# Hybrid trunk with routed experts: pair 2 is routed one phase ahead, hgrn groups start 20 slots apart, the router reads the unscaled residual, attention's steps stand two slots apart

## Chip, core and metric

One NeuronCore of a Trainium2 chip. The metric is the device time of one execution in microseconds (us), the median of several.

## What is computed

256 positions of 1024 float32 features pass through two layers, each a token mixer followed by a routed feed-forward (PEER), and a final RMSNorm.

```python
def reference(x, ...):
    h = x
    for i in range(2):
        xn = rmsnorm(h, mixer_norm[i])
        h = h + (swa_attention if i == 0 else hgrn2)(xn, ...)
        h = h + peer_ffn(rmsnorm(h, ffn_norm[i]), peer_w_q[i], peer_sub_keys[i], peer_u[i], peer_v[i])
    return rmsnorm(h, final_norm)

def peer_ffn(xn, w_q, sub_keys, u_tab, v_tab):        # per block of 128 positions
    q = (xb @ w_q).reshape(128, 8, 2, 128)             # 8 heads, 2 halves
    s = einsum('phcd,hckd->phck', q, keys)             # 128 scores per half
    sv, si = top_k(s, 16)
    cv, ci = top_k(sv[:, :, 0, :, None] + sv[:, :, 1, None, :], 16)   # of 16 x 16 sums
    expert = i1 * 128 + i2                             # indices picked by ci
    gates = softmax(cv)
    act = gelu(einsum('pd,phkd->phk', xb, u_tab[expert]))
    return einsum('phk,phkd->pd', gates * act, v_tab[expert])
```

So each position reads 8 x 16 = 128 experts per layer, each a u row and a v row. Attention is grouped-query with rotary positions and sinks; hgrn2 is a gated linear recurrence, here in 7 levels of doubling blocks.

## The kernel before

The 256 positions are two tiles of 128 (`TILES`). Work runs in four **phases** of 128 **slots** (`PER`). A slot `n` is one expert of each of the 128 rows of the phase's tile (phases 0 and 2: tile 0, layers 0 and 1; phases 1 and 3: tile 1).

The **foreground** of a slot goes through all engines. POOL (L386) issues an indirect DMA that gathers 128 rows of u and v (8 KB each) into one of the 8 slots of `ring`, once PE has freed slot n-8 (`slots_free`). DVE (L885) multiplies the u rows with `xn` and sums them up (`dots`); it waits for the landed gather. ACT takes gelu (L504), multiplies with the gate (`coef`) and makes a diagonal matrix (`diag`, L396). PE (L1212) multiplies that diagonal with the v rows and adds into `acc`, in two 512-wide matmuls, each run as two passes, so x4 in the trace. Then it increments `slots_free`.

**Beside** the foreground, each engine does the other work of the phase at written-out slot numbers: function `beside(p, q)` of each engine is called after `foreground` of slot q (on PE after that of slot q-1). Every engine is in order, so a wait in `beside` holds the foreground behind it. The other work is

- the *token mixer* of the other tile: attention in phase 0 (four groups, starts `ATTN_HEAD + 16 i`, step r of a group in slot start + r), hgrn in phases 1 and 2 (four groups, starts `HEAD + HGRN_PERIOD * i` = 8, 25, 42, 59). In a hgrn group PE projects at r = 0 to 13 (L1126 and L1130), ACT takes the sigmoid at r = 14 (L470), PE computes a level of scores at r = 16 to 23 (24 in phase 2, L1142), and the output projection runs at r = 33 to 36 (L1175). Weights come through `wmix`, issued by SP at r = 7, 14 (input, 2048 KB each) and 37 (output, 1024 KB).
- at `MIXED` = 96 DVE adds the mixer's output to `h` (`add_up`), the row is normalised (ACT squares, DVE `norm_ims`, ACT sqrt, DVE `norm_scale`), PE transposes `xn`, and ACT and DVE copy it to `xTs` (`norm_xT`).
- *routing* of the heads in five **units**: unit 0 is head 0, unit 1 head 1 (both routed in the last slots of the phase before), units 2, 3, 4 are pairs of heads. A unit is: PE projects (`route_project`, L1183, eight k-steps of 128x128 per column, a pair has four columns), ACT copies (`route_copy`), PE scores (L1202), DVE takes the top 16 per column (`top`), then the 256 sums, indices and gates (`candidates` to `gates`). `ROUTE_PE`, `ROUTE_SCORE`, `ROUTE_EXP`, `PAIR_DVE`, `HEAD_DVE` hold the slots. POOL waits for a head's indices (`r_done`) before its first gather. The routing weights of a unit (`wroute`, 2304 KB) are one buffer, reloaded by SP once the scores of the unit before are done (`load_route`).

At a phase boundary DVE adds `acc` to `h` in slot 1, once PE has done the last slot of the phase before; PE's first foreground waits for that (`h_ready`).

Before the phases stands a **prologue**: attention of tile 0, projections of tile 1 (`ahead`, from weights that lie in ring slots 0 to 5, so that gathers into these wait for it), the norm of tile 0 and the routing of units 0 and 1.

Of the kernel before, what the change touches and what calls it, by code (L numbers as in the profile page):

```python
# [13 lines left out]
P = 128  # L14
# [66 lines left out]
def trunk(nc, x, cos, sin, masks_attn, masks_hgrn, ident_in, iota_in, gains, mixer_gain, sinks, lb_raw, out_gain,  # L81
          attn_in, attn_out, hgrn_in, hgrn_out, route_w, experts, out):
    with ExitStack() as ctx:
# [16 lines left out]
        gainT = sb("gainT", [P, 2, KT])  # L100
# [17 lines left out]
        warm = sb("warm", [P, 2])  # L118

# [86 lines left out]
        xT_ps, xT_act, xT_dve, xT_mix = sem("xT_ps"), sem("xT_act"), sem("xT_dve"), sem("xT_mix")  # L206
# [67 lines left out]
        def rbank_of(u):  # L274
            return cbank if u % UNITS == 1 else rbank
# [10 lines left out]
        def _(sp):  # L286
# [60 lines left out]
            for p in range(PHASES):  # L347
                for q in range(PER):
                    if q == 10:
                        load_route(p, 2)  # L350
                    elif q == 26:
                        load_route(p, 3)
                    elif q == 50 and p == 1:
                        load_route(p + 1, 0)
                    elif q == 109 and p < 3:
                        load_route(p + 1, 1)
                    if p == 0:
                        if q == 37:
                            load_hgrn_in(0, 0, 0)
                        elif q == 69:  # L360
# [7 lines left out]
                    if q == 100 and p in (0, 2):  # L368
# [23 lines left out]
        def _(act):  # L392
# [95 lines left out]
            def route_copy(p, unit):  # L488
                u = unit_phase(p, unit) * UNITS + unit
                act.wait_ge(r_proj, u + 1)  # L490
                cols = scored(u)
                copy(rqT[:, cols], bands(rbank_of(u)[:], RHC)[:, cols]).then_inc(r_qT, 1)

            def route_exp(p, unit):
                u = unit_phase(p, unit) * UNITS + unit
                act.wait_ge(g_shift, u + 1)
                hs = heads_of(u)
                act.activation(ge[:, hs], cvs[:, hs], ACT.Exp).then_inc(g_exp, 1)
# [13 lines left out]
            def beside(p, q):  # L512
# [4 lines left out]
                elif q == 3 and p:  # L517
                    norm_sqrt(norm_at(p, 0))
# [858 lines left out]
```

## Time and profile before

| | us |
|---|---|
| runs shown, median (lowest, highest), 3 runs | 1582.83 (1579.26, 1584.77) |
| profiled execution | 1582.65 |
| its span, first to last instruction | 1580.6 |

| engine | busy us | share of the span |
|---|---|---|
| PE | 1380.6 | 87% |
| DVE | 1065.9 | 67% |
| ACT | 664.6 | 42% |
| POOL | 563.4 | 36% |

The DMA engines moved 628.01 MB, 397 GB/s over the span; the software queue with the gathers takes 82.5% of the 16 engines' time, SP's hardware queue 13.7%. In the page's 40 slices the DMA engines are at 9 tenths or more in all but the second and the last. How to read it: a share of the span is an average over stages with different limits, so the rows below go by stage. In a timeline row the columns are start, duration, engine, line, operation, and in brackets how long the engine had idled before it and who released it. An issue on POOL dates the release of the slot eight before.

### The profile page before, as it was taken

What the parts mean: (1) busy time and instruction counts of PE and PEld (TensorE: products, weight loads), DVE (VectorE), ACT (ScalarE), POOL (GpSimd) and SP (SyncE); (2) the same over time, 40 slices, a digit from 0 to 9 for tenths busy, and PEclk for the clock granted to TensorE, in tenths of its full rate; (3) what the DMA queues carried; (4) which work ended last, traced back from release to release, by engine and by line L of the source; (5) the groups of instructions that cost most, each with busy time, mean ns of one, the idle gap of its engine ahead of it and who ended that gap; (6) DMA issues with size and microseconds to landing.
All of it is one profiled execution on the core that took longest, in us unless ns stands there. A gap on an engine that the chain in (4) does not pass through costs nothing.

```text
span 1580.6 us, 15779 instructions
## 1 busy us (share of the span) xinstructions
PE 1380.6 (87%) x4918; PEld 739.3 (47%) x4918; DVE 1065.9 (67%) x2560; ACT 664.6 (42%) x1897; POOL 563.4 (36%) x518
## 2 busy tenths in 40 slices
PE   8899988878789989988878998999897888977776
PEld 5555554324246657543434665755452443422222
DVE  3369676665857677778585766688958585666644
ACT  3235445344443343454444334255444433344333
POOL 0033433444344223334433333242543344344441
PEclk9999998999999999999999999999999998999999
DMA  9099999999999999999999999999999999999995
GB/s 370 21 380 422 402 422 388 403 422 421 423 420 423 423 423 355 422 423 420 421 422 421 422 423 423 347 420 355 395 420 422 422 423 423 420 421 421 422 421 247
DMA packets 84051, 628.01 MB, mean 397 GB/s; under 512 B 9728, under 2 KB 10368, under 8 KB 13696
## 3 DMA queue, kind: packets, MB, share of 16 engines
q0 software_dynamic: 73728, 536.90, 82.5%
q1 hardware_dynamic: 9664, 89.87, 13.7%
q8 instruction: 38, 0.62, 0.2%
q10 hardware_dynamic: 576, 0.25, 0.1%
q14 instruction: 45, 0.37, 0.1%
HBM read 625.93 MB, written 1.05 MB: 397 GB/s over the span
## 4 chain that ended last, share of the span: by engine, by line
PE 44%; DMA 30%; DVE 13%; ACT 9%; issue 3%; POOL 0%; DVEq 0%; ACTq 0%; POOLq 0%
DMA ring<-experts,idx 30%; PE acc L1212 25%; DVE ring L885 7%; PE rbank L1183 5%; PE ab L1126 2%; PE ab L1130 2%; ACT L504 2%; PE acc L998 2%; PE y L1009 2%; ACT diag L396 1%; PE y L1175 1%; ACT coef L396 1%; PE cbank L1183 1%; ACT gel L504 1%; ACT L470 1%
## 5 line engine op out<-in xcount | busy, mean ns | idle before, releaser
L1212 PE MATMUL acc<-ring,diag 128*128 128x512 f32 x2048 | 994.5, 614 | 181.0 <-ACT diag L396 173.9
L386 POOL DMA_INDIRECT ring<-experts,idx x512 | 562.2, 1098 | 989.6 <-PE acc L1212 877.5
L885 DVE CUSTOM_DVE_ANT_0 ring<-ring,xn 128x1024 f32<-128x1024 f32 x512 | 624.3, 1223 | 302.5 <-DMA ring<-experts,idx 283.8
L1212 PEld LDWEIGHTS acc<-ring,diag 128*128 128x128 f32 x2048 | 362.6, 193 | 632.1 <-ACT diag L396 348.3
L504 ACT ACTIVATE gel<-dots 128x1 f32<-128x1 f32 x512 | 103.5, 202 | 770.0 <-DVE dots L885 769.2
L396 ACT ACTIVATE diag<-ident,coef 128x128 f32<-128x128 f32 x512 | 205.7, 402 | 16.8
L396 ACT ACTIVATE coef<-gate,gel 128x1 f32<-128x1 f32 x512 | 151.1, 295 | 16.6
L1183 PEld LDWEIGHTS rbank<-xTs,wroute 128*128 128x128 f32 x896 | 117.2, 193 | 49.2 <-issue 49.0
L1183 PE MATMUL rbank<-xTs,wroute 128*128 128x128 f32 x896 | 117.8, 276 | 0.9 <-DVE xTs L625 0.9
L1126 PEld LDWEIGHTS ab<-xTs,wmix 128*128 128x128 f32 x512 | 64.0, 192 | 10.5 <-issue 10.5
L1126 PE MATMUL ab<-xTs,wmix 128*128 128x128 f32 x512 | 67.6, 275 | 0.0
L1130 PE MATMUL ab<-wmix,xTs 128*128 128x256 f32 x256 | 63.1, 379 | 0.0
L504 ACT ACT_TABLE_LOAD x46 | 59.0, 1283 | 0.8
L1130 PEld LDWEIGHTS ab<-wmix,xTs 128*128 128x128 f32 x256 | 46.8, 190 | 15.6 <-issue 11.5
L885 DVE DVE_READ_ACCUMULATOR2_ANT dots<- 128x1 f32 x512 | 42.3, 83 | 0.0
L708 DVE TENSOR_TENSOR mix<-mix 128x512 f32<-128x512 f32 x48 | 33.2, 692 | 1.6
L1175 PE MATMUL y<-wmix,mix 128*128 128x512 f32 x64 | 33.0, 598 | 0.0
L998 PE MATMUL acc<-ring,xTs 128*128 128x384 f32 x96 | 32.5, 489 | 0.6 <-issue 0.6
L1009 PE MATMUL y<-wmix,mix 128*128 128x512 f32 x64 | 31.0, 597 | 0.5 <-ACT mix L396 0.5
L768 DVE MAX8 sv<-rbank 128x8 f32<-128x128 f32 x56 | 16.6, 296 | 20.8 <-PE rbank L1202 20.8
L1142 PEld LDWEIGHTS cbank<-mix 128*128 128x128 f32 x144 | 21.5, 192 | 15.3 <-issue 15.3
L724 DVE COPY_PREDICATED mix<-hmask,cbank 128x256 f32<-128x256 uint32 x32 | 14.1, 442 | 19.1 <-PE cbank L1142 13.8
(192 smaller groups left out, 916.0 us busy)
## 6 DMA issues: line engine op xcount, KB each, us to landing
wmix<-hgrn_in SPq DMA_DIRECT2D x16, 2048.0 KB
wroute<-route_w SPq DMA_DIRECT2D x14, 2304.0 KB
ring<-experts,idx POOLq DMA_INDIRECT x512
wmix<-hgrn_out SPq DMA_DIRECT2D x8, 1024.0 KB, 12.0
ring<-attn_in SPq DMA_DIRECT2D x3, 1536.0 KB, 8.6
wmix<-attn_out SPq DMA_DIRECT2D x4, 1024.0 KB, 10.1
ring<-attn_in SPq DMA_DIRECT2D x2, 768.0 KB, 8.4
gain<-gains SPq DMA_DIRECT2D x3, 512.0 KB
```

What stands on the lines that cost most here:

```text
L386: pool.indirect_dma_start(out=ring[:, k * 2 * D:(k + 1) * 2 * D], out_offset=None, in_=experts, in_offset=bass.IndirectOffsetOnAxis(ap=idx ...
L396: return act.activation(to, of, ACT.Copy, scale=scale)
L504: link(act.activation(gel[:, k:k + 1], dots[:, k:k + 1], ACT.Gelu))
L708: dve.tensor_tensor(to, hkq, sufpre, ALU.mult).then_inc(h_factors, 1)
L885: dve.tensor_tensor_reduce(out=u_rows(k), in0=u_rows(k), in1=xn[:, tile], scale=1.0, scalar=0.0, op0=ALU.mult, op1=ALU.add, accum_out=dots ...
L998: last = nc.tensor.matmul(to[:, 0:AW], xTs[:, side, k], w[:, k * AW:(k + 1) * AW], start=k == 0, stop=k == KT - 1)
L1009: last = nc.tensor.matmul(y[:, j * HALF:(j + 1) * HALF], a_oT[:, n % 2, c * P:(c + 1) * P], w[:, c * D + j * HALF:c * D + (j + 1) * HALF], ...
L1126: nc.tensor.matmul(ab[:, j, c * P:(c + 1) * P], w[:, k, c * P:(c + 1) * P], xTs[:, 0, k], start=k == 0, stop=k == KT - 1)
L1130: last = nc.tensor.matmul(ab[:, j, 256:512], xTs[:, 0, k], w[:, k, 256:512], start=k == 0, stop=k == KT - 1)
L1175: last = nc.tensor.matmul(y[:, j * HALF:(j + 1) * HALF], h_oT[:, c * P:(c + 1) * P], wmix[:, c, HIN + j * HALF:HIN + (j + 1) * HALF], star ...
L1183: last = nc.tensor.matmul(rbank_of(u)[:, c * P:(c + 1) * P], wroute[:, (k * RHC + c) * P:(k * RHC + c + 1) * P], xTs[:, 1, k], start=k == ...
L1212: last = nc.tensor.matmul(acc[:, j * HALF:(j + 1) * HALF], diag[:, n % DIAGS], v_rows(k)[:, j * HALF:(j + 1) * HALF], start=n % PER == 0, ...
```

## The change

- *Slots of the mixer.* `HGRN_PERIOD` goes from 17 to 20, so hgrn groups start at 8, 28, 48, 68, and `MIXED` from 96 to 105. Attention's steps, one slot apart before, get a slot between them (ATTN_PERIOD stays 16); its output and the transposed output go to bank `ab[:, 0]`, not `cbank`.
- *Routing one pair ahead.* Pair 2's projections move from slots 0 to 7 of their phase to slots 120 to 127 of the phase before (for phase 0: to the end of the prologue), with copy and scores in slots 0 and 1. Pair 3's move from 16 to 23 to 8 to 15, pair 4's from 40 to 47 to 23 to 27 and 45 to 47.
- *Unscaled residual.* PE transposes `h` itself, before the norm; DVE multiplies by the norm's gain while it copies to `xTs` (`gained`, with the two ffn gains added to `gainT`). The scale 1/rms, one number per position, doesn't change the order of the scores; it is kept in `rroute` and enters as `scale` of the exp in the gates and in `norm_scale` for `xn`. ACT's half of the copy (`norm_xT`) is gone.
- *Heads 0 and 1 in chunks.* The two columns of head 0 have banks, copies, scores and semaphore counts of their own, so that the first column's top can run while the second is projected. Head 1 uses `ab[:, 0]`.
- SP's routing loads move with their users: issued in slots 2, 18, 50 (phase 1), 116 (before 10, 26, 50, 109); the first hgrn loads in phase 0 in slots 49 and 81 (before 37 and 69).

```diff
-HGRN_PERIOD = 17
-MIXED = 96
+HGRN_PERIOD = 20
+MIXED = 105
-ROUTE_PE = (103, 105, 0, 16, 40)
-ROUTE_SCORE = (106, 108, 9, 25, 49)
-ROUTE_EXP = (111, 118, 17, 52, 74)
-PAIR_DVE = {2: tuple(range(10, 21)),
-            3: tuple(range(34, 40)) + tuple(range(51, 56)),
-            4: (56,) + tuple(range(68, 74)) + tuple(range(85, 89))}
-HEAD_DVE = {0: tuple(range(107, 114)), 1: tuple(range(114, 121))}
+CHUNKS = 6
+FIRST_CHUNK = (0, 2, 3, 4, 5)
+ROUTE_EXP = (115, 122, 13, 36, 61)
+PAIR_PE = {2: tuple(range(120, 128)), 3: tuple(range(8, 16)), 4: (23, 24, 25, 26, 27, 45, 46, 47)}
+PAIR_COPY = {2: 0, 3: 16, 4: 48}
+PAIR_SCORE = {2: 1, 3: 17, 4: 49}
+PAIR_DVE = {2: (3, 5) + tuple(range(8, 17)),
+            3: tuple(range(18, 23)) + tuple(range(34, 40)),
+            4: tuple(range(54, 63)) + (74, 75)}
+HEAD_DVE = {0: tuple(range(111, 118)), 1: tuple(range(118, 125))}
...
@@ load_route, SP @@
-                    sp.wait_ge(r_score, p * UNITS + (0, 2, 3, 4)[at_])
+                    sp.wait_ge(r_score, p * CHUNKS + (0, 3, 4, 5)[at_])
...
@@ attention on PE; ACT and DVE likewise @@
-                if r == 10:
+                if r == 11:
                     transpose_qk(n, ab[:, 1])
-                elif r == 12:
+                elif r == 15:
                     pe.wait_ge(a_qkT, n + 1)
...
-                elif r in (16, 17):
+                elif r in (22, 23):
                     pe.wait_ge(a_exp, n + 1)
...
@@ route_exp on ACT @@
-                act.activation(ge[:, hs], cvs[:, hs], ACT.Exp).then_inc(g_exp, 1)
+                act.activation(ge[:, hs], cvs[:, hs], ACT.Exp, scale=rroute[:, tile:tile + 1]).then_inc(g_exp, 1)
...
@@ route_begin on PE @@
+                if unit == 0 and c == 0:
+                    pe.wait_ge(xT_route, 2 * p + 2)
+                    pe.wait_ge(wroute_in, 16 * route_loads(p, 0))
+                    if p:
+                        pe.wait_ge(r_top, p * CHUNKS)
+                elif unit >= 2:
+                    pe.wait_ge(wroute_in, 16 * route_loads(p, unit - 1))
+                    pe.wait_ge(r_top, chunk_of(u, 0))
...
@@ beside on PE @@
-                if q in (MIXED + 4, MIXED + 5):
-                    transposes(norm_at(p, 1), tile, q - MIXED - 4, ab[:, q - MIXED - 4])
...
+                u = (p + 1) * UNITS
+                if q == MIXED + 1:
+                    pe.wait_ge(h_ready, evacuations(p) + 1)
+                    transposes(h[:, tile], 0, ab[:, 0])
+                    transposes(h[:, tile], 1, ab[:, 1])
+                elif q == MIXED + 3:
+                    route_project(u, 0, range(KT))
+                elif q == MIXED + 4:
+                    route_project(u, 1, range(KT))
+                elif q == MIXED + 5:
+                    route_scores(u, (0,))
+                elif q == MIXED + 6:
+                    route_scores(u, (1,))
+                elif q in (MIXED + 7, MIXED + 8):
+                    route_project(u + 1, q - MIXED - 5, range(KT))
+                elif q == MIXED + 10:
+                    route_scores(u + 1, (2, 3))
+                pair_projects(p + 1, 2, q)
...
@@ prologue on PE @@
-            ahead(0, range(0, 6))
-            transposes(2, 0, 0, ab[:, 0])
-            transposes(2, 0, 1, ab[:, 1])
-            route_begin(0)
-            for c in range(2):
-                route_project(0, c, range(KT))
-            route_scores(0)
-            for c in range(2, 4):
-                route_project(1, c, range(KT))
-            ahead(0, range(6, KT))
-            route_scores(1)
+            ahead(0, range(0, 2))
+            pe.wait_ge(h_ready, 1)
+            transposes(h[:, 0], 0, ab[:, 0])
+            transposes(h[:, 0], 1, ab[:, 1])
+            route_project(0, 0, range(KT))
+            route_project(0, 1, range(0, 4))
+            route_scores(0, (0,))
+            route_project(0, 1, range(4, KT))
+            ahead(0, range(2, 4))
+            route_scores(0, (1,))
+            for c in (2, 3):
+                route_project(1, c, range(KT))
+            ahead(0, range(4, KT))
+            route_scores(1, (2, 3))
             for g in range(1, ITERS):
                 ahead(g, range(KT))
+            for c in range(RHC):
+                route_project(2, c, range(KT))
+            route_scores(2, range(RHC))
```

## Rows read from the trace of the kernel before

**Rows 1.** The page: rate of each 39.5 us slice, then issues with median to landing.

```profile
GB/s 370 21 380 422 402 422 388 403 422 421 423 420 423 423 423 355 422 423 420 421 422 421 422 423 423 347 420 355 395 420 422 422 423 423 420 421 421 422 421 247
...
wroute<-route_w SPq DMA_DIRECT2D x14, 2304.0 KB
...
wmix<-hgrn_out SPq DMA_DIRECT2D x8, 1024.0 KB, 12.0
```

**Rows 2.** Stretches: length, busy PE, PEld, DVE, ACT, POOL, then PEclk, DMA share, GB/s.

```profile
80.00:100.00 20.00, 17.50 (x62) 10.46 (x60) 18.81 (x67) 5.67 (x12) 8.04 (x8) 1.00 0.91 357
...
160.00:180.00 20.00, 18.11 (x85) 10.71 (x84) 9.51 (x20) 10.74 (x32) 7.60 (x7) 1.00 0.97 385
...
270.00:290.00 20.00, 20.00 (x60) 10.17 (x59) 14.58 (x36) 8.38 (x28) 9.46 (x8) 0.91 0.86 320
...
600.00:630.00 30.00, 30.00 (x157) 21.22 (x156) 23.14 (x51) 10.77 (x32) 8.80 (x8) 1.00 0.89 337
...
990.00:1020.00 30.00, 30.00 (x160) 21.46 (x159) 19.91 (x40) 7.39 (x25) 7.99 (x7) 1.00 0.86 322
...
1060.00:1120.00 60.00, 56.87 (x223) 34.00 (x221) 50.94 (x131) 27.89 (x73) 21.41 (x20) 1.00 0.95 358
```

**Rows 3.** Timeline of POOL: issues after slots 39, 48 (phase 1), 39, 48, 88 (phase 2).

```profile
580.62 0.94 POOL L386 DMA_INDIRECT ring<-experts,idx  x1 [1.55 <-PE acc L1212]
...
622.08 1.03 POOL L386 DMA_INDIRECT ring<-experts,idx  x1 [2.09 <-PE acc L1212]
...
978.74 0.94 POOL L386 DMA_INDIRECT ring<-experts,idx  x1 [1.55 <-PE acc L1212]
...
1020.21 0.94 POOL L386 DMA_INDIRECT ring<-experts,idx  x1 [2.09 <-PE acc L1212]
...
1139.93 1.57 POOL L386 DMA_INDIRECT ring<-experts,idx  x1 [2.61 <-PE acc L1212]
```

**Rows 4.** Chain of waits, 575 to 640 us: start, length, what.

```profile
596.51 0.89 PE rbank L1183 x8
597.40 0.86 PE y L1175 x2
598.26 0.45 PE cbank L1142 x4
...
599.60 1.72 PE acc L1212 x4
...
615.77 1.30 PE ab L1130 x6
```

**Rows 5.** Timeline of PE: the foreground of slot 40, phase 1.

```profile
584.15 3.64 PE L1212 MATMUL acc<-ring,diag 128*128 128x512 f32 x4 [2.91 <-ACT diag L396]
```

**Rows 6.** Timeline of POOL in phase 0.

```profile
271.59 0.94 POOL L386 DMA_INDIRECT ring<-experts,idx  x1 [5.80 <-PE acc L1212]
```

**Rows 7.** Timeline of the prologue: residual add, first top, routing load, first gather.

```profile
64.10 1.22 DVE L628 TENSOR_TENSOR h<-h,y 128x1024 f32<-128x1024 f32 x1 [4.70 <-PE y L1009]
...
75.65 0.30 DVE L768 MAX8 sv<-rbank 128x8 f32<-128x128 f32 x1 [5.25 <-PE rbank L1202]
...
77.38 0.30 DVE L768 MAX8 sv<-rbank 128x8 f32<-128x128 f32 x1
...
80.89 0.33 SPq L304 DMA_DIRECT2D wroute<-route_w  x1
...
85.44 1.08 POOL L386 DMA_INDIRECT ring<-experts,idx  x1 [83.71 <-DVE idx L835]
```

**Rows 8.** Timeline behind the prologue: gelu's table load, first foreground, first refill.

```profile
97.71 1.28 ACT L504 ACT_TABLE_LOAD   x1
...
100.02 1.98 PE L1212 MATMUL acc<-ring,diag 128*128 128x512 f32 x4 [1.96 <-ACT diag L396]
...
102.28 0.94 POOL L386 DMA_INDIRECT ring<-experts,idx  x1 [2.25 <-PE acc L1212]
```

**Rows 9.** Timeline of PE: the first foreground of phase 1.

```profile
455.37 1.95 PE L1212 MATMUL acc<-ring,diag 128*128 128x512 f32 x4 [2.32 <-DVE h L628]
```

More of the change, by code:

```diff
@@ L118, in trunk @@
         warm = sb("warm", [P, 2])
+        rroute = sb("rroute", [P, TILES])
         idx = sb("idx", [P, TILES, PER], U32)
@@ L580, in _ @@
             norm_squares(2, 0)
-            norm_sqrt(2)
-            norm_xT(2, 1)
-            for unit in range(2):
-                route_copy(-1, unit)
+            norm_sqrt(2, rroute[:, 0:1])
+            route_copy(0, 0)
+            route_copy(0, 1)
+            route_copy(1, 2)
             stash_qkv(0)
-            for unit in range(2):
-                route_exp(-1, unit)
+            route_exp(0)
+            route_exp(1)
             for g in range(1, ITERS):
                 stash_qkv(g)
+            route_copy(2, 0)
             for p in range(PHASES):
@@ L615, in norm_plain, with gained @@
                 dve.tensor_scalar(xn[:, tile], h[:, tile], rstd[:], None, ALU.mult).then_inc(norm_done, 1)
-            def gained(k, side, layer, half, source):
+            def gained(k, side, row, half, source):
                 dve.wait_ge(xT_ps, 2 * k + half + 1)
@@ L823, in pick @@
             def pick(u):
-                cs = scored(u)
+                cs = slice(columns_of(u)[0], columns_of(u)[-1] + 1)
                 to = picks[:, cs].rearrange("p c (k a) -> p c k a", a=TOPK)
@@ L867, in route_head @@
                 if t < 2:
-                    top(u, scored(u).start + t)
+                    top(u, columns_of(u)[t])
                 elif t == 2:
@@ L927, in beside @@
                 elif q == MIXED + 2:
+                    gained(norm_at(p, 1), 1, 2 + (p + 1) // 2, 0, ab[:, 0])
+                    gained(norm_at(p, 1), 1, 2 + (p + 1) // 2, 1, ab[:, 1])
+                elif q == MIXED + 4:
                     norm_ims(norm_at(p, 1))
-                elif q == MIXED + 3:
-                    norm_scale(norm_at(p, 1), tile, (1, 2, 2)[p])
-                elif q == MIXED + 6:
-                    norm_xT(norm_at(p, 1), 1)
+                elif q == MIXED + 5:
+                    norm_scale(norm_at(p, 1), tile, rroute[:, tile:tile + 1], (1, 2, 2)[p])
                 for unit in range(2):
@@ L965, in _ @@
             add_up(0, y[:])
+            gained(2, 1, 2, 0, ab[:, 0])
+            gained(2, 1, 2, 1, ab[:, 1])
             norm_ims(2)
-            norm_scale(2, 0, 1)
-            norm_xT(2, 1)
+            norm_scale(2, 0, rroute[:, 0:1], 1)
             dve.wait_ge(late_in, 16 * len(LATE))
@@ L1204, in route_scores, with pair_projects @@
+            def route_scores(u, cs):
+                pe.wait_ge(r_qT, chunk_of(u, cs[0]) + 1)
+                for c in cs:
+                    last = nc.tensor.matmul(bank_of(u, c), rqT[:, c], wroute[:, (KT * RHC + c) * P:(KT * RHC + c + 1) * P], start=True, stop=True)
                 last.then_inc(r_score, 1)
+            def pair_projects(p, unit, q):
+                if q in PAIR_PE[unit]:
+                    s = PAIR_PE[unit].index(q)
+                    route_project(p * UNITS + unit, s // 2, range(s % 2 * 4, s % 2 * 4 + 4))
```

224 lines of the change are left out of this document (106 added, 118 removed).

## Prediction, before the change was built

> **What bounds the kernel now.** First the page's transfer rate by slice [rows 1]: wherever nothing disturbs them the 16 DMA engines run at 420 to 424 GB/s. One gather brings 128 rows of 8 KB, 1.049 MB, so 2.485 us at 422 GB/s; the 512 gathers alone are 1272 us. By the same division a routing load (2304 KB, 2.36 MB) costs 5.6 us, a hgrn input load 5.0 and a hgrn output load 2.5. Then the table of stretches [rows 2]: the rate falls only in a few places. Time lost to DMA is (422 - rate)/422 of a stretch: 80 to 100 us 3.1; 160 to 180 us 1.8; 270 to 290 us 4.8; 600 to 630 us 6.0; 990 to 1020 us 7.1; 1060 to 1120 us 9.1. The five behind the ramp sum to 28.8 us. In those of 600 and 990 PE is busy 30.00 of 30 us. So transfers bound the kernel, except where PE releases ring slots too slowly and the ring runs out of permits to gather. Before 80 us (no gathers) and after 1562 us (last slots, last norm) are fixed ends.
>
> How large a lag does the ring hide? The issue of gather n comes just after PE freed slot n-8, so the issues on POOL date PE's slots. From 580.62 (slot 39 freed) to 622.08 (slot 48) are nine slots of phase 1 in 41.5 us [rows 3]. The DMA engines had 9 x 2.485 plus an output load, 24.9 us of work, for them: a lag of 16.6, of which 6.0 were lost as above, so the ring hid 10.6. In phase 2 the same nine slots take 978.74 to 1020.21, 41.5 us; 7.1 lost, 9.5 hidden. I take 10. Behind them, 1020.21 to 1139.93, forty slots (49 to 88) take 119.7 us against 114.3 of DMA work (99.4, two input and two output loads); there the ring starts with no reserve, and 9.1 are lost [rows 2, 3].
>
> What fills those slots is read from the chain of waits [rows 4]: PE's cost at the margin is 1.72 us for a foreground (x4), 0.89 for a group of eight routing or hgrn products, 1.30 for one of six 256-wide ones, 0.86 for an output projection, 0.45 for a level of scores. Slots 40 to 48 hold 9 foregrounds 15.5, routing of pair 4 in eight slots 7.1, the output projection of hgrn group 0 3.4, 8 levels of group 1 3.6, projections of group 2 7.1: 36.7. The rest of the 41.5, 4.8, is the stall at slot 40: ScalarE runs sigmoid with two table loads, VectorE the first level, and PE waits 2.91 us for the next diag [rows 5].
>
> **The change, part by part.**
>
> (1) *hgrn period 20, pair 4 at slots 23 to 27 and 45 to 47.* Nothing is removed; work is moved apart. Slots 40 to 48 of phases 1 and 2 then hold 9 foregrounds 15.5, three routing steps 2.7, the output projection 3.4, two steps of group 1's projection 2.2, five levels 2.3, one step of group 2 0.9: 27.0. With the same stall of 4.8 they take 31.8. The DMA work is 22.4 + 5.0 + 2.5 = 29.9 (group 2's input load falls in here now). Lag 2 in place of 16.6: the 6.0 us of phase 1 go, and I keep 0.5, so **-5.5**. In phase 2 slots 49 to 88 hold by the same counting 114.2 us of PE work (before: 109.4, for 119.7 measured, so 10.3 of stalls, about two of the above). With these 124.5 against 114.3 of DMA work: a lag of 10.2, plus the 2 before, 12.2, of which the ring hides 10. About 2 us stay lost of 7.1 + 9.1 = 16.2: **-14.2**. In phase 1 the same slots have two more input loads, so nothing is lost there. What is late next is DMA itself. Bounds: 0 (stalls grow with the spread) to -22.2.
>
> (2) *Attention's steps spread, pair 2's routing out of slots 0 to 7.* In phase 0 the losses at 160 and 270 us, 6.6 together, come from in-line handovers: ScalarE is held by the exps between two table loads, PE waits for its diags, and POOL idles 5.80 us before the issue at 271.59 [rows 6]. With two slots between the steps the waits on ScalarE's copies vanish, but the exps with their loads stay in front of the diags. I take **-5.0**; bounds 0 and -6.6.
>
> (3) *Prologue, unscaled residual.* Before, the add that makes h ends at 65.32; squares, sqrt and scale follow, then transposes and products, and the first top starts at 75.65, the second 1.7 us later; head 0's indices give the first gather at 85.44; the routing load goes out at 80.89 [rows 7]. After, the transposes (about 1.1) start at 65.4, and the two gained multiplications, on VectorE like the copy they replace, end by 67.5. Column 0's 16 products take 1.8 (2 x 0.89), and its top overlaps column 1: its products, two steps of `ahead` and the scores end about 73.3, the second top about 75.1, where before it ended at about 79.1. First gather about 81.5, 3.9 earlier. The norm's squares, sqrt and scale now run beside the products and cost nothing: their first reader, the exp, waits for the top 16 anyway. Without that cover they would cost the 3.2 us that the transposes gain. But most of the 3.9 is not on the path: the routing load already keeps the DMA engines busy then, and it now waits for the third scores, about 80.3 (-0.6). The DMA engines have 8 gathers and this load, 25.5 us. At 357 GB/s their start in the stretch 80 to 100 is equivalent to 83.1 [rows 2], 2.2 behind the issue; now 82.5, so they run dry at 108.0. Before the loop PE now does 64 more products for pair 2 (8 x 0.89 = 7.1), and ScalarE's copy of them stands in its queue ahead of the first gelu with its table load. The three `ahead` blocks end at about 96.8 as before, the products at 103.9, the copy at 104.6, the table load (1.28) at 105.9; from there to the first foreground it was 1.0, so 106.9 in place of 100.02, and the first refill at 109.2 in place of 102.28 [rows 8]. Its data flow 2.2 later, 111.4: DMA stands still for 3.4 us. **+2.8**; bounds -0.6 (no gap at all) and +6.9 (the whole delay of the refill). The profile shows 1.28 us for the load, and gelu follows without a gap.
> The Trainium skill (ScalarE: Activation LUTs, What ACT_TABLE_LOAD costs) adds a drain of about 1.38 us to each switch, 2.66 in all; in this trace the foreground stands 2.31 us behind the load's start, with gelu, coef and diag in it, which leaves no room for a drain; with it the step would cost 1.4 us more.
>
> (4) *Pair 3 at slots 8 to 15, right behind pair 2.* PE at slot 8 now waits until pair 2's four tops are read; VectorE does them in slots 3, 5, 8 and 9, and it is in order. Counted from the end of the phase's add_up, VectorE needs about 8 x 1.3 + 4 x 1.73 (a top, [rows 7]) + 2.5 (norm, gained) = 19.8 us to the end of slot 9, PE 8 x 1.72 + 0.9 (scores) + 1.0 (transposes) = 15.7 to reach slot 8: a stall up to 5 us (lower bound 0, if both wait for gathers; below nothing is excluded, since a wait was added). Behind the waiting PE stand the foregrounds, so the releases, and slots 8 to 15 with two groups each, 28.7 us. Slots 0 to 15 sum to 44.4 + 5, against 39.8 + 5.6 of DMA: lag 4, under 10. The transition itself, where PE waits 2.32 for h [rows 9], is as before. I take **+1.0** for three boundaries, bounds 0 and +15.
>
> (5) *Routing loads nearer to their use*: issued after slot 115's and slot 17's scores, needed at 120 and 23. The nearest row is the 1024 KB output load, 12.0 us from issue to landing [rows 1]; this one is 2.25 times as large: from 12.0 to 16.8 + 2 (a third of the rate). Five foregrounds take PE at least 8.6 us, DMA-bound 12.4. A stall of 0 to 10, inside the ring's cover of 10: I take 0. It delays SP's later loads little, as they wait for later PE steps.
> The Trainium skill (DMA: Bandwidth & Descriptors, Queues, rings and completion order) says that each DMA engine goes round robin between its queues by packet: an even split gives an estimate of 11.2 us for the load. No row here times it, and by it the step stays at 0.
>
> (6) *The residual chain ends nine slots later* (MIXED 105) and head 0's indices are written in VectorE's slot 116, while gather 0 of the next phase needs them when slot 120 is freed, which needs VectorE's slot 120: order alone covers it. 0. The gain multiplications replace copies of equal length, `rroute` and the chunk semaphores: 0. Phase 3 has no idle of DMA (the last eight slices but one at 420 to 423 GB/s [rows 1]): 0.
>
> **Sum**: 1582.65 (the profiled execution's own time; span 1580.6, 2.0 around it, 0.2 under the median) - 5.5 - 14.2 - 5.0 + 2.8 + 1.0 = 1561.75, so **1561.8**. A second way: bytes after the ramp unchanged, losses 28.8 + 3.1 become about 3.1 + 0.5 + 2 + 1.6, and 3.4 and 1.0 come in: 11.6, which with the earlier start of 0.6 is again 20.9 less.
>
> **Rivals.**
> A. *Lag is moved, not removed*: the stalls of (4) and (5) come on top of dense slots 104 to 127 and 0 to 15, and each overshoots the ring's 10 us. For it: no slack is made, PE's work is the same. Against: per-phase PE work stays under DMA's. Four us at each of three boundaries give 1573.8.
> B. *It does not do what it says*: the idle DMA comes from ScalarE's and VectorE's chains, not from the crowding. Half-clock spells speak for it: PEclk 0.91 over 270 to 290 [rows 2]. Then (1) and (2) bring 3 and (3) costs 2.8: 1582.5.
> C. *Slower*: the crowded boundary. If the slot-8 wait and the late load both reach their full 5 and 10 us, on top of the lag of 4 to 6, the excess over the ring's 10 is 10 us at each of three boundaries: 1561.8 + 30 = 1592. It decides from 7 us of excess per boundary. Against it: at the boundary before, one wait of 2.32 us is all that PE has on the residual [rows 9], and the two new waits lie eight slots apart, with DMA-bound slots between.
> D. *All of it*: every loss goes and the prologue costs nothing, 1582.65 - 28.8 - 0.6 = 1553.3; a part of the forecast's own range.
>
> **How the numbers follow.** Forecast with D: 0.72, A 0.16, B 0.06, C 0.06. Range 1552 to 1577: from D to beyond A; it leaves out B, C and a little more. About 0.3% (4.7 us) is what a measurement of this kernel can tell from no change, so faster means under 1578: 0.72 + 0.16 and a little of B, 0.89; same 0.05; slower 0.06.
>
> **What would show it.** In the profile after: 420 to 424 GB/s through phase 1; in phase 2 at most a weak dip near slots 70 to 90; nine slots 40 to 48 in about 32 us; the first gather at about 81.5 but the first foreground at about 107, with a DMA gap of about 3 us behind 108; a wait of PE at slot 8 for VectorE. Wrong it would be if dips stand at the boundaries (A, C), or if dips stay inside the hgrn stretch though slots 40 to 48 are short (B).

## The result, and the profile after

| | before | after |
|---|---|---|
| median, 5 runs each (lowest, highest), us | 1582.83 (1579.26, 1584.77) | 1573.54 (1570.06, 1575.87) |
| ratio after/before, 95% interval | | 0.9941 (0.9919 to 0.9963) |
| profiled execution, its span, us | 1582.65, 1580.6 | 1573.54, 1571.7 |

The change makes the kernel 9 us faster (5.9 to 12.8 by the interval). The forecast was 1561.8, 21 us faster: the direction is right, less than half of the gain is there, and the time lies in the range of 1552 to 1577. The question is where the other 12 us went.

The same table of stretches as [rows 2], of the changed kernel: length, busy time of PE, PEld, DVE, ACT, POOL, then PEclk, DMA share, GB/s.

```profile
80.00:100.00 20.00, 20.00 (x97) 14.09 (x96) 15.54 (x53) 2.31 (x6) 7.66 (x8) 1.00 0.98 404
...
170.00:190.00 20.00, 20.00 (x86) 11.47 (x85) 10.73 (x23) 11.54 (x35) 9.12 (x9) 1.00 0.97 378
280.00:300.00 20.00, 20.00 (x63) 10.15 (x62) 10.96 (x21) 8.80 (x29) 10.11 (x9) 0.94 0.86 317
490.00:510.00 20.00, 20.00 (x100) 14.08 (x99) 9.33 (x18) 7.36 (x19) 6.44 (x5) 1.00 0.89 332
600.00:630.00 30.00, 28.01 (x132) 18.57 (x131) 21.55 (x51) 8.04 (x27) 8.73 (x9) 1.00 1.01 421
880.00:910.00 30.00, 30.00 (x150) 21.14 (x149) 17.28 (x42) 10.46 (x28) 8.73 (x8) 0.95 0.82 307
990.00:1020.00 30.00, 29.17 (x144) 19.17 (x144) 25.79 (x55) 11.03 (x35) 12.79 (x10) 1.00 1.01 420
1060.00:1120.00 60.00, 57.32 (x230) 34.89 (x229) 41.33 (x87) 26.51 (x74) 18.98 (x21) 1.00 1.01 418
1110.00:1150.00 40.00, 36.26 (x114) 18.39 (x113) 33.30 (x71) 20.39 (x58) 17.14 (x16) 1.00 1.00 408
1260.00:1290.00 30.00, 29.73 (x116) 17.75 (x116) 23.41 (x63) 11.97 (x34) 11.30 (x10) 0.91 0.99 390
```

And two stretches of the kernel before, at the places of the new dips:

```profile
490.00:510.00 20.00, 20.00 (x98) 13.54 (x97) 15.61 (x39) 7.80 (x20) 9.04 (x7) 1.00 1.01 422
880.00:910.00 30.00, 28.91 (x134) 19.45 (x133) 24.20 (x69) 10.75 (x31) 10.19 (x10) 1.00 1.01 423
```

The stretches of 600 and 990 us, at 337 and 322 GB/s before, now run at 421 and 420. In their place there are new dips at 490, 880 and 1260 us: slots 8 to 16 or so of phases 1, 2 and 3. By the rule of the prediction, (422 - rate)/422 of a stretch, the time lost is

| where | before | after |
|---|---|---|
| ramp, 80 to 100 us | 3.1 | 0.9 |
| attention, phase 0 (160 and 270 before, 170 and 280 after) | 6.6 | 7.1 |
| slots 8 to 16 (490, 880, 1260) | 0 | 4.3 + 8.2 + 2.3 = 14.8 |
| inside the hgrn stretch | 22.2 | 1.3 (1110 to 1150) |

The sum behind the ramp falls from 28.8 to 23.2 only.

### The profile page after: what moved, and what is told of

Read it like the earlier page. It is cut to its first block, busy times and chain, and to the rows that moved or that the text cites. A ratio compares the mean times of both kernels' runs of the same rounds, so it can differ in the third digit from the quotient of the medians.

```text
span 1571.7 us, 15776 instructions
## 1 busy us (share of the span) xinstructions
PE 1384.2 (88%) x4918; PEld 748.0 (48%) x4918; DVE 1066.1 (68%) x2564; ACT 664.5 (42%) x1897; POOL 563.5 (36%) x518
## 3 DMA queue, kind: packets, MB, share of 16 engines
q1 hardware_dynamic: 9664, 89.87, 13.8%
## 4 chain that ended last, share of the span: by engine, by line
PE 43%; DMA 32%; DVE 15%; ACT 7%; issue 2%; POOL 0%; DVEq 0%; ACTq 0%; POOLq 0%
DMA ring<-experts,idx 32%; PE acc L1230 25%; DVE ring L897 7%; PE rbank L1197 4%; PE ab L1138 3%; PE ab L1142 2%; PE acc L1010 2%; ACT diag L410 1%; ACT L516 1%; PE y L1021 1%; ACT coef L410 1%; PE ab L1197 1%; ACT gel L516 1%; DVE si L781 1%; DVE si L784 1%
## 5 line engine op out<-in xcount | busy, mean ns | idle before, releaser
L1230 PEld LDWEIGHTS acc<-ring,diag 128*128 128x128 f32 x2048 | 366.7, 194 | 599.0 <-ACT diag L410 300.6
L1197 PEld LDWEIGHTS rbank<-xTs,wroute 128*128 128x128 f32 x832 | 109.8, 196 | 62.8 <-issue 56.7
L1197 PE MATMUL rbank<-xTs,wroute 128*128 128x128 f32 x832 | 111.4, 280 | 15.2 <-DVE si L784 11.6
## 6 DMA issues: line engine op xcount, KB each, us to landing
wroute<-route_w SPq DMA_DIRECT2D x14, 2304.0 KB, 12.7
ring<-experts,idx POOLq DMA_INDIRECT x512, 15.1
wmix<-hgrn_out SPq DMA_DIRECT2D x8, 1024.0 KB, 12.3
```

What stands on the lines that cost most here:

```text
L1197: last = nc.tensor.matmul(bank_of(u, c), wroute[:, (k * RHC + c) * P:(k * RHC + c + 1) * P], xTs[:, 1, k], start=k == 0, stop=k == KT - 1)
L1230: last = nc.tensor.matmul(acc[:, j * HALF:(j + 1) * HALF], diag[:, n % DIAGS], v_rows(k)[:, j * HALF:(j + 1) * HALF], start=n % PER == 0, ...
```

## The experiments

Times are medians, with the ratio to the kernel before, which was measured beside them on the same chip. Its level was 1582.8 us beside the result above, then 1579.5 (e1 to e4), 1580.4 (the change once more, e5 to e7) and 1581.6 (e8, e9). So kernels are compared by ratio. The expectations of e1 to e4 were written when only the first level was known; the last column puts each run on it (ratio x 1582.83).

| run | us | ratio to before (95% interval) | at the first level, us |
|---|---|---|---|
| the change, once more | 1573.67 | 0.9955 (0.9937 to 0.9973) | 1575.7 |
| e1, period 19 alone | 1569.61 | 0.9934 (0.9917 to 0.9951) | 1572.4 |
| e9, period back at 17 | 1584.23 | 1.0020 (1.0008 to 1.0031) | 1586.0 |
| e2, tops early | 1564.56 | 0.9897 (0.9875 to 0.9919) | 1566.5 |
| e3, pair 3 light | 1564.99 | 0.9903 (0.9886 to 0.9920) | 1567.5 |
| e5, pair 3 spread | 1565.83 | 0.9905 (0.9887 to 0.9922) | 1567.8 |
| e4, attention dense | 1574.88 | 0.9972 (0.9953 to 0.9991) | 1578.4 |
| e7, tops early, phase 0 | 1562.66 | 0.9886 (0.9868 to 0.9903) | 1564.8 |
| e8, all three | 1565.86 | 0.9902 (0.9886 to 0.9919) | 1567.3 |
| e6, load late (one run) | 1570.95 | | |

**The base line.** Changed kernel, run once more. 

> The changed kernel once more, beside the others of this call, as their base line: 1570 to 1574 us, about 9 us under the kernel before, whatever the theory.

The same 7 to 9 us. But the two profiled executions of this one kernel differ, and their spans are 1571.7 and 1566.4. In the second the stretches read:

```profile
170.00:190.00 20.00, 20.00 (x86) 11.42 (x85) 13.77 (x30) 13.09 (x41) 8.02 (x8) 1.00 1.01 421
280.00:300.00 20.00, 20.00 (x67) 10.35 (x66) 12.38 (x25) 9.24 (x30) 11.32 (x10) 1.00 0.98 384
490.00:510.00 20.00, 20.00 (x103) 14.33 (x102) 7.63 (x20) 4.55 (x15) 6.71 (x6) 1.00 0.93 363
880.00:910.00 30.00, 30.00 (x155) 21.13 (x154) 15.73 (x39) 9.03 (x24) 9.20 (x10) 1.00 0.90 339
1260.00:1290.00 30.00, 27.63 (x107) 15.11 (x105) 24.17 (x69) 12.26 (x34) 13.62 (x13) 1.00 1.01 408
```

The dip of 170 us isn't there, that of 280 loses 1.8 us in place of 5.0, and slots 8 to 16 lose 2.8 + 5.9 + 1.0 = 9.7 in place of 14.8. So below a dip counts by its place, and a difference of some 30 GB/s between two single profiles counts for nothing; the time counts by its interval.

### Is it the spread of the hgrn groups?

e1 is the kernel before with the groups 19 slots apart, and nothing else of the change but what must follow it.

```diff
-HGRN_PERIOD = 17
-MIXED = 96
-ROUTE_PE = (103, 105, 0, 16, 40)
-ROUTE_SCORE = (106, 108, 9, 25, 49)
-ROUTE_EXP = (111, 118, 17, 52, 74)
+HGRN_PERIOD = 19
+MIXED = 102
+ROUTE_PE = (109, 111, 0, 16, 40)
+ROUTE_SCORE = (112, 114, 9, 25, 49)
+ROUTE_EXP = (117, 124, 17, 54, 76)
...
-            3: tuple(range(34, 40)) + tuple(range(51, 56)),
-            4: (56,) + tuple(range(68, 74)) + tuple(range(85, 89))}
-HEAD_DVE = {0: tuple(range(107, 114)), 1: tuple(range(114, 121))}
+            3: tuple(range(34, 40)) + tuple(range(53, 58)),
+            4: (58, 59, 60) + tuple(range(72, 80))}
+HEAD_DVE = {0: tuple(range(113, 120)), 1: tuple(range(120, 127))}
```

> The kernel before with only the hgrn groups spread (period 19, MIXED 102, routing as before: pair 2 at slots 0 to 7, pair 3 at 16 to 23, pair 4 at 40 to 47; heads 0 and 1 and VectorE's steps moved to match). Theory S (the idle DMA in the hgrn stretches of before is PE's crowding): slots 40 to 48 take 32.3 + 4.8 = 37.1 us against 29.9 us of DMA work, lag 7, under the ring's 10, so nearly all of the 22.2 us goes: 1561 to 1567 us. Rival P (it is pair 4's routing at 40 to 47 that must go): the dips at slots 40 to 48 stay, 1575 us or more.

Measured 1569.61, 0.66% faster than before, at the first level 1572.4: more than rival P allows, and 5 us short of theory S. Its stretches:

```profile
480.00:510.00 30.00, 29.20 (x135) 19.29 (x135) 24.61 (x75) 10.04 (x28) 11.45 (x10) 1.00 1.01 424
600.00:630.00 30.00, 30.00 (x154) 21.00 (x153) 23.50 (x52) 11.15 (x35) 10.69 (x10) 1.00 1.02 423
880.00:910.00 30.00, 29.05 (x137) 19.70 (x136) 23.99 (x66) 10.92 (x31) 9.54 (x10) 1.00 1.01 423
1000.00:1030.00 30.00, 30.00 (x151) 20.77 (x150) 24.85 (x56) 15.34 (x41) 10.67 (x10) 1.00 0.98 389
1060.00:1120.00 60.00, 57.80 (x222) 34.52 (x221) 51.92 (x123) 29.08 (x77) 22.65 (x20) 1.00 1.00 407
```

At 600 us it runs at 423 in place of 337; of the 16.2 us of phase 2, 2.3 and 2.1 stay. And where the changed kernel dips at 490 and 880 us it runs at 424 and 423: those dips don't come from the spread. Besides, e1 alone is as fast as the whole change (0.9934 against 0.9941 and 0.9955): no run here shows a net gain in time from the other parts.

e9 undoes this part in the changed kernel (`HGRN_PERIOD = 17`, one line). 

> The changed kernel with the hgrn period back at 17 (MIXED stays 105, the routing of the change stays). Theory S (the spread of the groups is what removed the dips inside the hgrn stretch): slots 40 to 48 take 32.3 + 4.8 = 37.1 us against 24.9 us of DMA work, lag 12, and the forty slots behind are as crowded as before, so 8 to 12 us of loss come back: 1579 to 1584 us. Rival Q (pair 4's move away from slots 40 to 44 did it): 1570 to 1575 us.

Measured 1584.23, slower than the kernel before. The spread is worth 0.65% here, 10 us, inside the 8 to 12 that were expected to come back, with pair 4's routing away from slots 40 to 44 in both: rival Q falls for the time. For the dips at slots 40 to 48 it doesn't: there e9 loses 1.1 and 1.8 us (600 and 990 us), the kernel before 6.0 and 7.1, and by POOL's issues the nine slots of phase 1 take 36.5 us, before 41.5. Either step, the spread (e1) or pair 4's move (e9), takes most of these two dips away. What comes back without the spread stands behind slot 49 of phase 2, 11.7 us:

```profile
600.00:630.00 30.00, 30.00 (x154) 20.98 (x154) 19.77 (x44) 9.82 (x35) 8.04 (x9) 1.00 0.99 407
990.00:1020.00 30.00, 30.00 (x145) 20.26 (x143) 22.11 (x46) 7.78 (x27) 8.93 (x8) 1.00 0.97 397
1060.00:1120.00 60.00, 55.85 (x216) 33.36 (x215) 45.46 (x96) 28.01 (x73) 24.63 (x19) 0.97 0.93 340
```

### What is lost at slots 8 to 16?

The timeline of the changed kernel at the start of phase 1, POOL, SP, DVE and PE, has start, length, engine, line, operation, operands, and in brackets the wait before it. Issues on POOL date the release of slots 0, 6, 7 and 8 (455.70, 474.21, 475.93, 485.23).

```profile
455.70 1.40 POOL L400 DMA_INDIRECT ring<-experts,idx  x1 [2.42 <-PE acc L1230]
456.35 0.33 SPq L318 DMA_DIRECT2D wroute<-route_w  x1
...
468.10 1.23 DVE L897 CUSTOM_DVE_ANT_0 ring<-ring,xn 128x1024 f32<-128x1024 f32 x1 [4.95 <-DMA ring<-experts,idx]
470.38 5.28 PE L1230 MATMUL acc<-ring,diag 128*128 128x512 f32 x8 [4.59 <-ACT diag L410]
473.19 1.23 DVE L897 CUSTOM_DVE_ANT_0 ring<-ring,xn 128x1024 f32<-128x1024 f32 x1 [0.64 <-DMA ring<-experts,idx]
474.21 1.01 POOL L400 DMA_INDIRECT ring<-experts,idx  x1 [7.65 <-PE acc L1230]
475.93 0.94 POOL L400 DMA_INDIRECT ring<-experts,idx  x1 [0.70 <-PE acc L1230]
...
479.03 1.13 PE L1197 MATMUL rbank<-xTs,wroute 128*128 128x128 f32 x8 [3.38 <-DVE si L784]
480.00 1.53 PE L1138 MATMUL ab<-xTs,wmix 128*128 128x128 f32 x8
481.32 3.13 PE L1230 MATMUL acc<-ring,diag 128*128 128x512 f32 x4
...
485.23 1.20 POOL L400 DMA_INDIRECT ring<-experts,idx  x1 [8.36 <-PE acc L1230]
```

Relieved of pair 2, PE runs through the landed slots 0 to 5 at about 1.7 us each and then stands: DVE waits 4.95 us for gather 6, since SP's routing load, issued at 456.35, takes its turn in the transfers: from slot 3's dots at 455.07, which had waited for their gather, to slot 6's at 468.10 are 13.0 us, as long as three gathers and this load (7.5 + 5.6). Then DVE and PE follow the landings, and nothing is left over from PE's quick slots. Now comes slot 8: PE waits 3.38 us for pair 2's last top, its first matmuls run slow (the foreground 3.13 us, in later slots 1.88), and it has two groups of products in each of eight slots. From 475.93 (slot 7) to 510.02 (slot 15) eight slots take 34.1 us, where the transfers need 19.9: a lag of 14.2 against the ring's 10, and 4.3 lost. In phase 2 the same slots take 35.4 us, so the lag is 15.5, but 8.2 are lost: the ring hid 7.3 there, and why not 10 is open.

The slow matmuls are a matter of PE's granted clock, and they don't always come. Over 480 to 490 us it is 0.83 in this execution (part of it at 1.2 GHz, the rest at 2.4) and 1.00 in the other, where the wait is 3.18 us and the foreground behind it takes 1.88. There the eight slots take 32.2 us, and 2.8 are lost in place of 4.3. This execution first, then the other:

```profile
480.00:490.00 10.00, 10.00 (x51) 7.05 (x50) 9.76 (x31) 4.00 (x13) 2.36 (x2) 0.83 1.01 416
```

```profile
480.00:490.00 10.00, 10.00 (x59) 7.37 (x59) 9.76 (x26) 5.83 (x14) 2.88 (x3) 1.00 1.01 419
```

Three kernels take away a piece each. **e2** moves only the last two tops:

```diff
-PAIR_DVE = {2: (3, 5) + tuple(range(8, 17)),
+PAIR_DVE = {2: (3, 5, 6, 7) + tuple(range(10, 17)),
```

> The changed kernel with the last two tops of pair 2 on VectorE in slots 6 and 7, not 8 and 9, so that PE at slot 8 waits for no later slot of VectorE. Theory T (at the boundary the wait of 3.4 us and eight slots of 3.5 us in a row add up to more than the ring hides): part of the 14.6 us returns, as VectorE's work up to slot 7 grows by what slots 8 and 9 lose: 1566 to 1571 us. Rival W (the wait alone costs it): all returns, 1559 to 1562 us. Rival D (density alone): no change, 1572 to 1575 us.

Measured 1564.56, at the first level 1566.5: theory T, 7 to 9 us faster than the change. The wait of slot 8 is no more: in its timeline PE's products start without one. The stretches of 490 and 880 us run at 406 and 400 in place of 332 and 307. The row of the timeline, then the two stretches:

```profile
475.18 1.05 PE L1197 MATMUL rbank<-xTs,wroute 128*128 128x128 f32 x8
```

```profile
490.00:510.00 20.00, 20.00 (x99) 13.94 (x98) 10.20 (x26) 6.05 (x17) 6.63 (x6) 1.00 0.99 406
880.00:910.00 30.00, 30.00 (x148) 20.83 (x147) 20.34 (x55) 10.47 (x29) 9.69 (x9) 1.00 0.99 400
```

**e3** leaves the wait and makes the slots light:

```diff
-                    route_project(p * UNITS + unit, s // 2, range(s % 2 * 4, s % 2 * 4 + 4))
+                    ks = range(s % 2 * 4, s % 2 * 4 + 4)
+                    if unit == 3:
+                        ks = (0,) if s % 2 == 0 else (KT - 1,)
+                    route_project(p * UNITS + unit, s // 2, ks)
```

> The changed kernel, pair 3's projections cut to two of eight k-steps (k 0 and 7), in the same slots 8 to 15 and behind the same wait; the rest of pair 3's projection is left out, so its experts are others, as many. Each of these slots costs PE 0.67 us less, 5.4 us per phase. Theory T: the lag over slots 8 to 15 falls from 14.6 to 9.2, under the ring's 10, so the losses at the boundaries go nearly all: 1560 to 1564 us. Rival W (the wait): at most 2 us faster, 1571 to 1574 us.

Measured 1564.99, the same gain, though PE still waits 3.13 us in slot 8; at the first level that is 1567.5, 3 us over theory T. So neither alone is the cause: rival W falls here, rival D fell with e2, and what stands is that wait and dense slots add up (T). The wait in the timeline of e3, then its two stretches:

```profile
477.94 0.46 PE L1197 MATMUL rbank<-xTs,wroute 128*128 128x128 f32 x2 [3.13 <-DVE si L784]
```

```profile
490.00:510.00 20.00, 20.00 (x89) 13.14 (x88) 12.75 (x36) 7.18 (x21) 7.82 (x7) 1.00 1.02 428
880.00:910.00 30.00, 30.00 (x133) 19.82 (x132) 21.17 (x57) 10.64 (x30) 11.76 (x11) 1.00 0.99 384
```

**e5** leaves no work out and spreads it:

```diff
-ROUTE_EXP = (115, 122, 13, 36, 61)
+ROUTE_EXP = (115, 122, 13, 41, 63)
-PAIR_PE = {2: tuple(range(120, 128)), 3: tuple(range(8, 16)), 4: (23, 24, 25, 26, 27, 45, 46, 47)}
-PAIR_COPY = {2: 0, 3: 16, 4: 48}
-PAIR_SCORE = {2: 1, 3: 17, 4: 49}
+PAIR_PE = {2: tuple(range(120, 128)), 3: (9, 11, 13, 15, 17, 19, 21, 22), 4: (38, 39, 40, 42, 43, 45, 46, 47)}
+PAIR_COPY = {2: 0, 3: 23, 4: 48}
+PAIR_SCORE = {2: 1, 3: 24, 4: 49}
...
-            3: tuple(range(18, 23)) + tuple(range(34, 40)),
-            4: tuple(range(54, 63)) + (74, 75)}
+            3: tuple(range(34, 43)) + (54, 55),
+            4: tuple(range(56, 63)) + (74, 75, 76, 77)}
...
@@ SP, third routing load of a phase @@
-                    elif q == 18:
+                    elif q == 25:
```

> The changed kernel, pair 3's eight projection steps in slots 9, 11, 13, 15, 17, 19, 21 and 22, not 8 to 15; its scores at 24, tops from 34; pair 4's projections at 38 to 40, 42, 43, 45 to 47. Nothing left out. Theory T (crowding of slots 8 to 15 behind a short wait): the excess over slots 8 to 15 falls by four steps, 3.6 us, and the wait of slot 8 goes, so the losses of 4 and 8 us at the boundaries go nearly all: 1560 to 1565 us. Rival H (crowding comes back at 38 to 47, where the output projection stands too: nine slots 40 to 48 with five routing steps and group 1's last projections): dips there, 1568 to 1573 us.

Measured 1565.83, 0.9905 against 0.9955 of the change measured beside it; 423 and 408 GB/s at 490 and 880 us. So the losses at the boundaries go, as T says. But the time is over T's 1565, at the first level 1567.8, and new losses stand elsewhere, as H says: 4.5 us at 1080 to 1120 and 2.6 at 150 to 170. The change loses 0.5 and 0.2 there.

The length of slots 8 to 15 (from POOL's issues; the transfers need 19.9 us) and the time lost in the stretches of 490 and 880 us, side by side:

| kernel | slots 8 to 15, phases 1 and 2, us | lost, us |
|---|---|---|
| before | 22.5 and 22.6 | 0 and 0 |
| the change | 34.1 and 35.4 | 4.3 and 8.2 |
| the change, once more | 32.2 and 34.5 | 2.8 and 5.9 |
| e2, tops early | 28.8 and 28.8 | 0.8 and 1.6 |
| e3, pair 3 light | 26.8 and 27.4 | 0 and 2.7 |
| e5, pair 3 spread | 25.4 and 25.2 | 0 and 1.0 |

By and large, the longer the slots, the more is lost. But the ring's 10 us is no sharp edge: e3 loses 2.7 at a lag of 7.5, and in phase 3 the change loses 2.3 at a lag of 7.3 (27.2 us).

### Attention's spacing

**e4** is the changed kernel with attention's steps at r = 10 to 26 as before (the numbers of all three engines, banks as changed). 

> The changed kernel with attention's steps back at their slots of before (banks as changed). Theory N (the spacing brings nothing: the trace after still loses 7 us near 180 and 290 us, where before it lost 6.6): 1571 to 1576 us, the same. Rival A (the spacing brings about 5 us and something else takes them back): 1577 to 1580 us.

Measured 1574.88, in N's range; but the ratio, 0.9972 against 0.9955 and 0.9941 of the change, makes it 1578.4 at the first level, in A's. That is 3 to 5 us slower than the change, with intervals that overlap, and the change wasn't measured beside it. The rates settle it no better: over the stretches of 140, 170 and 280 us e4 loses 5.1 us, the change 7.3 in one execution and 3.5 in the other. So it is open whether the spacing brings nothing or up to 5 us.

**e7** is e2 with another place for pair 4 in phase 0:

```diff
@@ against e2; ScalarE and VectorE use these two in phase 0 @@
+PAIR_DVE_0 = {**PAIR_DVE, 4: (56, 57, 58, 61, 63, 65, 66, 68, 69, 70, 72)}
+ROUTE_EXP_0 = (115, 122, 13, 36, 67)
```

> e2 (pair 2's tops early), and in phase 0 alone VectorE's steps of pair 4 at slots 56 to 58, 61, 63, 65, 66, 68 to 70 and 72, with the gates' exp at 67: out of the slots of the last attention group's mask (59, 60), and away from its exps at 62. Theory V (spreading attention's steps brought nothing since pair 4's steps and the gates' exp, moved to 54 to 62, meet the last group's on VectorE and ScalarE): the dip at 280 to 300 us, 5 us, goes: 4 to 5 us faster than e2. Rival E (the exps with their two table loads alone do it, wherever pair 4 is): the dip stays, as e2.

The dip of 280 us is gone, against rival E. The dip of 170 us is gone too, but not by this edit: the first slot that it changes is 54, at 247 us, and in the second execution of the changed kernel that dip wasn't there either. Whether VectorE's steps or the gates' exp made the dip of 280 us was not separated. The rows of e7 stand first, e2's behind:

```profile
280.00:300.00 20.00, 19.51 (x59) 9.19 (x57) 14.92 (x30) 8.92 (x29) 12.37 (x10) 1.00 1.01 420
170.00:190.00 20.00, 20.00 (x80) 10.98 (x79) 13.64 (x33) 11.88 (x36) 9.89 (x8) 1.00 1.01 421
```

```profile
280.00:300.00 20.00, 20.00 (x64) 10.17 (x63) 11.28 (x22) 8.88 (x30) 10.28 (x9) 0.96 0.89 336
170.00:190.00 20.00, 20.00 (x86) 11.36 (x85) 11.28 (x26) 11.06 (x34) 7.63 (x8) 1.00 0.96 368
```

But the ratio only goes from 0.9897 to 0.9886, with intervals that overlap: the 4 to 5 us expected are not shown in the time. At 490 us e7 runs at 367 GB/s where e2 had 406, at 880 at 375 where e2 had 400, with slots 8 to 15 as long as in e2, 28.8 us. That some of the gain came back there is possible, but two executions of the changed kernel differ by as much (332 and 363, 307 and 339). **e8** joins e5's spread to it. 

> The changed kernel with the three edits together: pair 2's tops early (e2), pair 3 spread over slots 9 to 22 (e5), pair 4's steps and exp moved in phase 0 alone (e7). Theory T and V: no dip in phase 0 and none at the boundaries, only 4 to 5 us at slots 70 to 90 of phase 2 left: 1557 to 1561 us, the fastest. Rival G (a dip that is taken away comes back later, as from e2 to e7, since the ring is no reserve that lasts): 1562 to 1566 us, as e2, e5 and e7.

1565.86, no better than e2 or e5 alone: as rival G forecast, the gains don't add. With 412 and 422 GB/s at 490 and 880 us it has other dips, at 150 to 170, 800 to 810 and 1080 to 1120 us (2.7, 2.9 and 5.6 us). G's reason is shown only in part. The first and the last of these dips stand in e5 too (2.6 and 4.5), so they can as well come from e5's placing of pairs 3 and 4, its rival H. For G speaks that e2 loses 3.7 us at 1080 to 1120, where the changed kernel, with the same steps in these slots, lost 0.5 and 0.8. Why 800 is among them was not followed up. e7 is the fastest kernel measured, 1562.66 us, 1.1% under the kernel before and 0.7% under the change measured beside it.

### The prologue

**e6** delays the load that SP issues at 103.45 us in the changed kernel.

```diff
                     if q == 2:
+                        if p == 0:
+                            sp.wait_ge(slots_free, 2)
                         load_route(p, 2)
```

> The changed kernel, but the second routing load of phase 0 waits until PE has freed two ring slots, some 6 us later. Theory L (behind the prologue there is no gap in the transfers because this load, 5.6 us of DMA work issued at 103.45 us, stands in for the gathers that PE's pair 2 holds back): between 104 and 114 us the rate falls from 421 GB/s by 3 to 4 us worth of transfers. Rival M (the refills come early enough by themselves): no dip there.

The rows of e6, then those of the changed kernel over the same stretches:

```profile
104.00:108.00 4.00, 3.41 (x5) 1.35 (x6) 3.90 (x11) 3.30 (x13) 0.00 (x0) 0.60 0.54 225
108.00:112.00 4.00, 4.00 (x11) 1.85 (x10) 3.86 (x13) 1.89 (x7) 2.48 (x2) 0.97 0.45 143
```

```profile
104.00:108.00 4.00, 3.47 (x5) 1.55 (x6) 3.90 (x11) 3.25 (x13) 0.00 (x0) 0.62 1.07 441
108.00:112.00 4.00, 4.00 (x10) 1.68 (x10) 3.86 (x13) 1.94 (x7) 2.49 (x2) 0.96 0.96 405
```

The gap of 4.5 us ((422-225)/422 x 4 + (422-143)/422 x 4) appears when the load is late: theory L. What the gap costs in time a single run, 1570.95, can't show: runs of the changed kernel spread from 1568.2 to 1575.9.

## Why the prediction was right or wrong

*What bounds the kernel*: right. The gains and losses that were traced to a place, in this and the other kernels, are ones of the transfer rate there.

*(1) Period 20, pair 4 moved*: right in mechanism, and in size as far as the rates go. Forecast -19.7, from the rates -20.9. Slots 40 to 48 of phase 1, 31.8 us forecast, took 609.42 - 580.97 = 28.4 (POOL's issues in the changed kernel's timeline, below). In time only 10 us are shown each for e1 (the spread alone) and for e9 against the change (the spread, with pair 4 moved in both). No run holds the spread and pair 4's move together and nothing else, so whether the kernel's time gets all of the 20 us is not shown.

```profile
580.97 1.30 POOL L400 DMA_INDIRECT ring<-experts,idx  x1 [1.82 <-PE acc L1230]
...
609.42 0.94 POOL L400 DMA_INDIRECT ring<-experts,idx  x1 [2.51 <-PE acc L1230]
```

*(4) Pair 3 at slots 8 to 15*: the mis-sized term that made the forecast wrong. Forecast +1.0, measured +14.8 in one execution, just inside its own bounds of 0 to 15, and +9.7 in the other. The wait was foreseen (up to 5 us; it was 3.4) and so was the work of slots 8 to 15 (28.7 us). The error is the stretch over which the sum was made, "Slots 0 to 15 sum to 44.4 + 5, against 39.8 + 5.6 of DMA: lag 4". That lets the 5.6 us of the routing load and PE's quick slots 0 to 7 pay for slots 8 to 15. They can't: by slot 6 PE had caught up with the landings and stood waiting, the load was already being moved, and what an engine spares while it waits for data isn't kept. The right sum starts where DVE has last waited for a gather (slot 8's, 473.19) and PE has freed slot 7: 28.7 + 3.4 + 2.0 (slow matmuls) - 19.9 = 14.2, over the ring's 10. e2 takes the wait out of this sum and e3 a part of the work, and most of the loss goes with either. The second fault is the ring's 10 itself: taken from slots 40 to 48 of the kernel before, it was 9.9 in phase 1 but 7.3 in phase 2. That makes 2.6 of the 3.9 us that phase 2 lost more, and the reason is open.

*(3) Prologue*: wrong in sign. Forecast +2.8, measured about -2.6: the transfers start at 80.5 in equivalent, not 83.1 (first routing load at 78.98, before 80.89; 404 GB/s in the ramp, 0.9 us lost, and 15 GB/s already from 70 to 80 us, worth 0.4). The chain was near (first gather 80.5 for 81.5, first refill 108.22 for 109.2), but the gap of 3.4 us isn't there. The step left out one DMA of those that move: with pair 2's scores done ahead, the *next* routing load goes out at 103.45, in front of the gap. e6 shows it.

*(2) Attention*: forecast -5.0, measured +0.5 in the profiled execution and about -3 in the other one (1.9 lost in the same two stretches, and 1.7 at 140 to 160 us, where it ran at 387 GB/s). What is left is mostly the dip of 280 us: pair 4's steps moved into slots 54 to 62, and the gates' exp to 61, right onto the last group's mask at 59 and 60 and exps at 62. That VectorE and ScalarE are shared by two written-out lists was not looked at. e7 shows this dip go when they are parted. What the spacing by itself is worth, 0 to 5 us, e4 leaves open.

*(5) Loads nearer to their use*: right. They land 12.7 us after issue (median), inside 12.0 to 18.8, and PE's wait at slot 8 is for VectorE. PE waits for such a load once, at slot 120 of phase 1, inside the 0 to 10 forecast, and the transfers ran at 422 GB/s there:

```profile
826.35 1.16 PE L1197 MATMUL rbank<-xTs,wroute 128*128 128x128 f32 x8 [2.69 <-DMA wroute<-route_w]
```

*(6)*: right, the first gathers of phases 1 to 3 wait for no indices. One later gather does, that of slot 80 of phase 1, for 2.35 us.

With the four terms as measured in the one profile, 1582.65 - 20.9 + 0.5 - 2.6 + 14.8 = 1574.5, against 1573.54. Two other misses cancel by luck: (2) brought 5.5 us less than forecast and (3) 5.4 more. The 12.7 us between 1561.8 and 1574.5 are then (4)'s 13.8 less 1.2 of (1).

The rivals: A, given 0.16, is what happened at (4), but not evenly over the three boundaries (4.3, 8.2, 2.3); nothing was lost at slots 104 to 127, and nothing by the loads of (5), which A also names. That its 1573.8 is so near to the time rests on the same luck. C's mechanism is A's; its late load of 10 us didn't come. B falls with e1 and e9: the spread is worth 10 us, not 3.

## What to carry to other kernels

Where a ring of buffers couples engines to transfers, start a sum of excess work at the last moment at which the consumer waited for data, and end it at the peak; idle time before that is not credit, and a load that is already under way isn't either. Take the time that the ring hides as a range, here 7 to 10 us, and not as an edge. When steps are moved, list for each engine what else is written for the same slots, and for each queue what the move lets go earlier: here the first left the dip of 280 us in place (1.8 to 5.0 us), and the second closed a gap of 4.5. And gains of single dips didn't add here (e8); that a ring hands what it hid to the next crowded place is a likely reason, not a shown one.

## What the runs showed that was not expected

While the transfers run at 420 to 424 GB/s, SP's loads of this kernel take nearly the same time to land whatever their size. The changed kernel's issues, with the median time to landing at the end:

```profile
wmix<-hgrn_in SPq DMA_DIRECT2D x16, 2048.0 KB, 11.9
wroute<-route_w SPq DMA_DIRECT2D x14, 2304.0 KB, 12.7
ring<-experts,idx POOLq DMA_INDIRECT x512, 15.1
wmix<-hgrn_out SPq DMA_DIRECT2D x8, 1024.0 KB, 12.3
```

1024 KB take 12.3 us and 2304 KB 12.7; a gather of 1024 KB from the other queue takes 15.1. That is the time of six gathers at 2.485 us (14.9), as if it stood behind those issued earlier; no run separates this.
